# Causal and window masks of nine passes of a first attention layer added by VectorE, with a changed order of normalising

## The reference, cut to what matters

```
def masked_softmax(s, mask, sink=None):
    s = jnp.where(mask, s, -jnp.inf)
    m = jnp.max(s, axis=-1, keepdims=True)
    ...
    e = jnp.where(mask, jnp.exp(s - m), 0.0)
    den = jnp.sum(e, axis=-1, keepdims=True)
    ...
    return e / jnp.where(den > 0, den, 1.0)
```

## Time and profile before

| | us |
|---|---|
| median of three runs | 763.97 |
| lowest and highest | 763.23, 764.12 |
| the profiled execution | 764.18 |
| its span | 762.4 |

### The profile page before, as it was taken

One profiled execution on the slowest core, in us unless ns is written; L12 is line 12 of the kernel. 1 busy time (PEld: TensorE's weight loads), 2 busy tenths in 40 slices (PEclk: granted clock), 3 DMA queues, 4 the chain that ended last, 5 costly groups with the idle time before them and its releaser, 6 DMA issues.

```text
span 762.4 us, 12229 instructions
## 1 busy us (share of the span) xinstructions
PE 745.4 (98%) x5039; PEld 641.5 (84%) x5039; DVE 497.9 (65%) x685; ACT 380.3 (50%) x577; POOL 25.6 (3%) x43
## 2 busy tenths in 40 slices
PE   5999999999999999999999999999999999999998
PEld 3687876478888878788999999999878999999886
DVE  1486769638847757884889999647863735546431
ACT  2564476545354756545543444697453544344330
POOL 3000001001000000013000000000000000000000
PEclk9999999999999999999999999999999999999999
DMA  9995348914366373353745554514453654454511
GB/s 367 422 380 184 153 172 326 400 70 144 123 237 242 111 262 126 111 204 117 273 172 185 197 191 166 192 58 138 152 183 135 229 214 183 152 219 173 213 56 55
DMA packets 21959, 146.50 MB, mean 192 GB/s; under 512 B 2589, under 2 KB 2717, under 8 KB 5393
## 3 DMA queue, kind: packets, MB, share of 16 engines
q1 hardware_dynamic: 20880, 142.62, 50.4%
q0 software_dynamic: 752, 2.06, 0.9%
q10 hardware_dynamic: 272, 1.05, 0.3%
HBM read 144.68 MB, written 1.05 MB: 191 GB/s over the span
## 4 chain that ended last, share of the span: by engine, by line
PE 78%; DVE 2%; issue 2%; ACT 0%; POOL 0%; POOLq 0%; DVEq 0%; ACTq 0%
PE banks L456 23%; PE banks L458 22%; PE banks L457 22%; PE banks L550 3%; PE banks L639 1%; PE banks L574 1%; DVE WL L1686 1%; PE banks L678 1%; PE banks L646 1%; PE banks L923 0%; PE banks L908 0%; PE banks L682 0%; DVE KT L1718 0%; PE banks L927 0%; PE banks L925 0%
## 5 line engine op out<-in xcount | busy, mean ns | idle before, releaser
L1686 DVE TENSOR_TENSOR WL<-RAW,WH 128x2048 fp32r<-128x2048 f32 (+1 forms) x103 | 233.6, 2278 | 60.2 <-ACT WH L1170 59.9
L1170 ACT ACTIVATE WH<-RAW 128x2048 fp32r<-128x2048 f32 (+1 forms) x103 | 195.7, 1906 | 72.6 <-PE banks L458 65.6
L456 PE MATMUL banks<-HH,WH 128*128 128x256 f32 x768 | 217.9, 284 | 0.0
L457 PE MATMUL banks<-HL,WH 128*128 128x256 f32 x768 | 217.3, 283 | 0.0
L458 PE MATMUL banks<-HH,WL 128*128 128x256 f32 x768 | 217.3, 283 | 0.0
L457 PEld LDWEIGHTS banks<-HL,WH 128*128 128x128 f32 x768 | 147.3, 192 | 0.1
L456 PEld LDWEIGHTS banks<-HH,WH 128*128 128x128 f32 x768 | 147.3, 192 | 0.1
L458 PEld LDWEIGHTS banks<-HH,WL 128*128 128x128 f32 x768 | 147.3, 192 | 0.0
L456 PE MATMUL banks<-WH,HH 128*128 128x512 f32 (+1 forms) x320 | 127.7, 399 | 1.9 <-DVE WL L1686 0.8
L458 PE MATMUL banks<-WH,HL 128*128 128x512 f32 (+1 forms) x320 | 124.6, 389 | 0.0
L457 PE MATMUL banks<-WL,HH 128*128 128x512 f32 (+1 forms) x320 | 124.5, 389 | 0.0
(11 more groups left out here) (295 smaller groups left out, 910.6 us busy)
## 6 DMA issues: line engine op xcount, KB each, us to landing
RAW<-in_weights_dram SPq DMA_DIRECT2D x114, 1024.0 KB, 4.8
BIG<-in_weights_dram SPq DMA_DIRECT2D x6, 1024.0 KB, 6.2
ROTS<-in_weights_dram SPq DMA_DIRECT2D x4, 1024.0 KB, 7.2
PROBS<-in_weights_dram SPq DMA_DIRECT2D x2, 1024.0 KB, 11.6
RAW<-in_weights_dram SPq DMA_DIRECT2D x2, 816.0 KB, 10.3
GATE<-in_weights_dram SPq DMA_DIRECT2D x3, 512.0 KB, 9.7
X<-in_x_dram ACTq DMA_DIRECT2D x1, 1024.0 KB, 6.0
QT<-in_weights_dram SPq DMA_DIRECT2D x1, 1024.0 KB, 13.7
```

Source lines behind the costliest of these rows:

```text
L456: pe.matmul(out_, lhsT=w[0], rhs=x[0], start=start, stop=False, **more)
L457: pe.matmul(out_, lhsT=w[0], rhs=x[1], start=False, stop=False, **more)
L1170: do(act.activation(WH[:, home[n], 0:kb * width], RAW[:, slot[n] % RAW_RING, 0:kb * width], ACT.Copy), high_done)
L1686: do(dve.tensor_tensor(WL[:, home[n], w], RAW[:, slot[n] % RAW_RING, w], WH[:, home[n], w], ALU.subtract), low_done)
```

## The change

`by_vector(p)` is true for all passes but 4, 5 and 6. In those passes TensorE issues no mask matmuls: the second score matmul of each unit closes the bank. VectorE, ahead of the minimum, adds a constant of 1e30 or zero to the two diagonal blocks of both banks (128x512) in place in PSUM, and in a window pass also to the block behind the diagonal of the second half (128x256), and waits for the adds to complete. In steps 8 to 11 of layer 0, VectorE normalises pass i - 1 ahead of the minimum of pass i; in the other steps behind it, as before.

Further: `low_stick(3)` stands ahead of the split `lows(branch_first + 7)`. In front of the feed-forward VectorE makes both splits of fi0 ahead of `low_banks(3, 0)`, the first of fi1 between the two `add_merged` of the second half and the second of fi1 ahead of `stat_merged(1)`; ScalarE makes both splits of fi1 ahead of `square("n3", 1)`; TensorE turns the second half of the norm in the middle of `hidden_tokens(1, 0)` and not ahead of it.

```diff
--- before.py
+++ after.py
@@ -449,6 +449,9 @@
         block = ctx.enter_context(nc.Block())
 
 
+        def by_vector(p):
+            return p not in (4, 5, 6)
+
         @block.tensor
         def _(pe):
             def product(out_, w, x, start, stop, **more):
@@ -636,10 +639,13 @@
                         q, k = x["q"], x["k"]
                         kb = q // 2 if k is None else k
                         out_ = bank[:, 0:P] if t == 0 else bank[:, P:TRI]
-                        pe.matmul(out_, lhsT=half_of(q, QT, q // 2, t * P, (t + 1) * P),
-                                  rhs=half_of(q, KT, kb, 0, (t + 1) * P), start=(t == 0), stop=False)
-                if p == 0:
-                    pe.wait_ge(mask_set, 1)
+                        mm = pe.matmul(out_, lhsT=half_of(q, QT, q // 2, t * P, (t + 1) * P),
+                                       rhs=half_of(q, KT, kb, 0, (t + 1) * P), start=(t == 0), stop=(by_vector(p) and t == 1))
+                        if by_vector(p) and t == 1:
+                            ps.fill(mm, f"s.{u}")
+                if by_vector(p):
+                    return
+                pe.wait_ge(mask_set, 1)
                 for u, bank in zip(pair, banks):
                     window = units[u]["mask"] == "window"
                     diagonal = bank[:, 0:TRI].rearrange("p (b c) -> p b c", b=3)[:, 0:3:2, :]
@@ -991,7 +997,7 @@
             pe.wait_ge(mt_low, 4)
             output(2)
 
-            def hidden_tokens(i, t):
+            def hidden_tokens(i, t, between=None):
 
                 for half in range(2):
                     wait_parts(pe, f"fi{i}", half)
@@ -1000,6 +1006,8 @@
                 bank = ps.open(pe, "proj", use)
                 out_ = bank[:, :].rearrange("p (u c) -> p u c", u=2)
                 for k in range(KB):
+                    if between and k == KB // 2:
+                        between()
                     mm = product(out_, [h[:, k, t * P:(t + 1) * P] for h in (HH, HL)],
                                  [w[:, slot_:slot_ + 2, k * 256:(k + 1) * 256] for w in (WH, WL)], k == 0, k == KB - 1)
                 ps.fill(mm, use)
@@ -1013,8 +1021,7 @@
 
             normed(3, 0)
             hidden_tokens(0, 0)
-            norm_turn(3, 1)
-            hidden_tokens(1, 0)
+            hidden_tokens(1, 0, lambda: norm_turn(3, 1))
             normed(3)
             hidden_tokens(0, 1)
             hidden_tokens(1, 1)
@@ -1604,11 +1611,10 @@
             square("n3", 0)
             highs(first_split("fi0") + 2)
             high_norm(3, 0)
-            highs(first_split("fi1") + 1)
+            highs(first_split("fi1") + 2)
             for c in range(2):
                 ps.wait_drained(act, f"y2.1.{c}")
             square("n3", 1)
-            highs(first_split("fi1") + 2)
             high_norm(3, 1)
 
             def silu_tokens(i, t):
@@ -1845,6 +1851,14 @@
                 for u in (2 * p, 2 * p + 1):
                     ps.wait_filled(dve, f"s.{u}")
                 h = units[2 * p]["sink"]
+                if by_vector(p):
+                    diagonal = both_scores[:, :, 0:TRI].rearrange("p u (b c) -> p u b c", b=3)[:, :, 0:3:2, :]
+                    mask = const("maskw")[:, 0:P].unsqueeze(1).unsqueeze(1).to_broadcast([P, 2, 2, P])
+                    do(dve.tensor_tensor(diagonal, diagonal, mask, ALU.add))
+                    if units[2 * p]["mask"] == "window":
+                        behind_ = const("maskw")[:, P:2 * P].unsqueeze(1).to_broadcast([P, 2, P])
+                        do(dve.tensor_tensor(both_scores[:, :, P:S], both_scores[:, :, P:S], behind_, ALU.add))
+                    do.after()
                 do(dve.tensor_reduce(NM[:, pair, 0], both_scores[:, :, 0:P], AX.X, ALU.min))
                 do(dve.tensor_reduce(NM[:, pair, 1], both_scores[:, :, P:TRI], AX.X, ALU.min),
                    peaks_got if h is None else None)
@@ -1902,9 +1916,12 @@
             def attention(layer, extra):
                 a, b = spans[layer]
                 for i in range(a, b + 4):
+                    short = layer == 0 and i > 7
+                    if short and i - 1 < b:
+                        normalise(i - 1)
                     if i < b:
                         peaks(i)
-                    if a <= i - 1 < b:
+                    if not short and a <= i - 1 < b:
                         normalise(i - 1)
                     if a <= i - 3 < b:
                         heads_out(layer, i - 3)
@@ -2276,8 +2293,8 @@
             conf(2)
             low_stick(2)
             conf(3)
+            low_stick(3)
             lows(branch_first + 7)
-            low_stick(3)
             lows(branch_first + 8)
             fence[0] = FENCES["branches"]
 
@@ -2311,15 +2328,14 @@
             stat_merged(0)
             dve.wait_ge(ffnr_in, 16)
             gained_hat("n3", 0, FFNR)
-            lows(first_split("fi0") + 1)
+            lows(first_split("fi0") + 2)
             low_banks(3, 0)
-            lows(first_split("fi0") + 2)
             add_merged(1, 0)
+            lows(first_split("fi1") + 1)
             add_merged(1, 1)
-            lows(first_split("fi1") + 1)
+            lows(first_split("fi1") + 2)
             stat_merged(1)
             gained_hat("n3", 1, FFNR)
-            lows(first_split("fi1") + 2)
             low_banks(3, 1)
 
             def gate_tokens(i, t, n):
```

## The result

The changed kernel takes 765.72 us (median of 6 runs, 765.25 to 766.67), the kernel before beside it 763.6; the ratio is 1.0033, interval 1.0021 to 1.0044. So it is 0.33% slower, just over what such a measurement can tell from no change, and just above the end of my range (765.3). The profiled execution took 765.81, its span is 764.0.

A forecast was written before the change was run, and what follows sets the result against it. TensorE, busy 745.4 of 762.4 us, was taken as the bound, with VectorE work free only where nothing waits for it. The terms summed to -0.95 us, giving 763.0 us, range 761.2 to 765.3.

The forecast's parts named there:

- the sum: Whole kernel: 3.1 - 0.6 - 2.1 - 0.55 - 0.8 = -0.95 us against the kernel before.
- steps (a) to (e): Passes 0 to 3: chain passing each add's delay on until TensorE is 3.1 us late at the compressed scores.
- What a mask costs either engine: Each moved mask: TensorE saves 0.23 (causal) or 0.40 (window); VectorE's adds cost 0.73 or 1.06 us.
- layer 1: Passes 12 to 19: VectorE waits for TensorE there, so the adds are hidden and 2.1 us is gained.
- the choice of 0.23 over 0.34: Causal pass: 0.23 us saved on TensorE, not 0.34, because the first full product behind a differently tiled group is slow.
- Passes 0 to 3: First four passes, two masks each: VectorE's adds make the minimum late and the kernel 3.1 us longer.
- Passes 7 to 11: Later passes of layer 0: step 7 loses 0.3, steps 8, 10 and 11 gain, 9 nothing; -0.6 us.
- Branch outputs: ato.0 to ato.2: low_stick(3) ahead of a split removes a 1.1 us loss, of which 0.55 is kept.
- Norm before the feed-forward: Reordered splits and turn remove two TensorE waits (0.6 and 0.5); a later silu wait costs 0.3; -0.8 us.
- The third: Short steps 7 to 11 each wait for exponentials, and window passes absorb nothing: 766.2 us; chance 0.10.
- The first (adds hidden): Adds of passes 0 to 3 are hidden after all, -1.6 instead of +3.1: 758.3 us; chance 0.07.
- the second: All ends favourable outside passes 0 to 3, 0.34 saved per mask, ato keeps 1.1: 761.8 us; chance 0.23.

The follow-up runs named there:

- e13: Changed kernel with dummy transposes in TensorE's waits at the turns of passes 0, 1, 2, 5 and 6 and inside pass 2's turn: 762.87 us, ratio 0.9988.
- e3: Kernel before with only the masks of passes 0 to 3 moved to VectorE: 769.74 us, ratio 1.0071.
- e4: Kernel before with only pass 3's mask moved to VectorE: 765.95 us, ratio 1.0029.
- e2: Changed kernel with the masks of passes 0 to 3 back on TensorE: 758.47 us, ratio 0.9934.
- the tail alone: Kernel before with only the edits behind layer 1 (low_stick(3), the splits of fi0 and fi1, the moved turn): 762.04 us, ratio 0.9982.
- e11: Kernel before with 10 dummy transposes ahead of the turn of pass 6, where there was hardly a wait: 764.18 us, ratio 1.0013.

## Why the prediction failed

**The step that failed is the sum.** It added lateness and savings, each at full clock, and priced TensorE's waits at their own length. It had no term for what waits do to the granted clock: 3.0 us in the profiled execution. One line even shut it out: "As matmuls are only removed, a loss in TensorE's own time is excluded." The matmuls left took longer. By executions it is 765.7 against e13's 761.4 at full clock, 4.3, of which 1.6 are a further stretch as the profiled execution of the kernel before also has it (there from 161.6 on, from 167.0 after). I had the means: my own steps (a) to (e) said that TensorE would be idle ahead of the compressed scores, and the page of the profile shows the granted clock in a row of its own. The Trainium skill, "TensorE: Matmul & The Clock Gate", section What's actually happening, says of this clock that "the default state is throttled, and activity releases the throttle"; the windows above agree: 1.70 of 4 us busy, then 0.5. By that rule the prediction would have needed a rival "half clock behind the waits"; with what the trace shows of it, 3.0 less the 0.5 of step 6, that rival stands at 763.0 + 2.5 = 765.5. The stretch at 161.6 of the kernel before, with TensorE busy ahead of it, is not explained by that sentence.

**What a mask costs either engine**: right. Window adds 0.69 and 0.42, 1.06 with the wait. A causal add is 0.70, and 0.73 with the wait. At full clock layer 1 alone gave 2.2 for 2.1; in the trace of the changed kernel its eight passes take back 0.25, 0.28, 0.24, 0.24, 0.43, 0.24, 0.24 and 0.25, 2.2 in all. Seven of the eight lie between 0.24 and 0.28, so the choice of 0.23 over 0.34 holds: the product behind the mask comes 0.35 sooner, and its successor gives 0.1 of that back. The eighth is pass 16, with 0.43 as put; passes 7 to 10, with conditioning behind them too, saved 0.43 or 0.44 each. Only the pass with transposes behind it gave 0.28 for 0.31.

**Passes 0 to 3**: right, +3.17 for +3.1, by the steps as told. Where TensorE loses the time is only partly as told: 0.76 ahead of the rotated block's product at 82.22 and 0.39 at the turn of pass 0 instead of 0.7 ahead of the scores of pass 2; 0.82 at the turn of pass 1 for about 1; and 1.89 at that of pass 2 for about 1, since what the masks no longer cost TensorE comes out as waiting there. Nothing was to be regained in passes 4 to 6, but step 6 takes back 0.4 to 0.5 in the three traces with a slow stretch at 112 and no dummies (changed, e3, e4). E3 gave the whole chain (compressed scores at 111.25; 766.8 with one stretch of 3.4 us, 2.6 over the kernel before with one), e4 its last link, e2 its absence.

**Passes 7 to 11**: -0.67 in the trace, -0.6 alone at full clock, for -0.6. Step 7 gave +0.34 (the turn of pass 6 waits 0.74), step 8 -0.44, 10 -0.36, 11 -0.25. Step 9 came out at 0.04: it gained 0.43 and lost 0.47 to this wait, for the score bank:

```profile
153.44 0.93 PE L642 MATMUL banks<-KT,QT 64*128 64x128 f32 x8 [0.41 <-ACT PROBS L1294]
```

**Branch outputs**: -0.75 in the trace of the changed kernel, -0.53 in those of e2 and e13, for -0.55, by the mechanism told. The wait for the transformed block has gone, which gives 1.2, and ato.2 starts 0.67 later than it could. The bracket says "issue", but VectorE's read of ato.0's bank ends at 542.86, 0.1 ahead of the start. The 0.2 by which the traces differ come in the products behind it, and why isn't shown.

```profile
542.17 0.69 DVE L2265 SCALAR_TENSOR_TENSOR ROTS<-BIG,banks 128x512 f32<-128x512 f32 x1
```

```profile
542.24 0.28 PE L461 MATMUL banks<-AL,WL 128*128 128x256 f32 x1
542.96 0.36 PE L459 MATMUL banks<-AL,WH 128*128 128x256 f32 x1 [0.44 <-issue]
```

**Norm before the feed-forward**: -0.66 for -0.8. Both waits have gone, 1.2 for the 1.1 that I had put. The silu's bank is late instead, 0.62 between starts where 0.23 is usual, and the product behind it starts 0.1 later still: 0.5 for 0.3. With the branch outputs that is -1.4 for -1.35, as the tail alone gave.

```profile
582.89 0.39 PE L461 MATMUL banks<-WH,HL 128*128 128x512 f32 x1
583.51 0.47 PE L459 MATMUL banks<-WH,HH 128*128 128x512 f32 x1 [0.23 <-DVE ZT L2345]
```

**The rivals.** The third names 766.2, near the result, but mostly by a mechanism that did not happen: its wait for the exponentials came in one step, 9, while steps 8, 10 and 11 gained, and passes 0 to 3 absorbed what I said. That its number is near is luck. The first (adds hidden) and the second are out by the compressed scores and by the layer 1 rows.

**The range** was built from the ends of known terms. A whole term was missing, and all of it lies on one side.

## What to carry to other kernels

Where a change makes the busiest engine wait in a cluster, price the waits twice: their length, and the time at half clock that may follow; take the waits of one place together, not only the longest, and look at the granted clock behind them in the trace of an experiment. A part-by-part undo pays here: the same change without its four worst passes is 0.66% faster than the kernel before. And moving work to an engine with spare time helps only in the steps in which its result isn't what the next engine waits for.

## What the runs showed of the hardware that I had not expected

TensorE's granted clock fell to half behind waits that were each short: 0.39, 0.82, 1.89 and 0.41 us in the changed kernel (rows above), and 1.01 and 0.41 in e4. It then stayed there for some 6.8 us in the first case and about 3.4 in the second, although TensorE was busy throughout. Equal waits don't give equal stretches: e3 was busy for the same 1.70 of 4 us ahead, and its profiled execution has 3.4 us at half clock there and not 6.8. A stretch of 3.4 costs about 1.6 us (762.6 and 764.2 of the kernel before). The same program meets it in some executions and not in others, and one such stretch appeared in the kernel before directly behind TensorE at work without a gap. Dummy transposes in a wait kept the clock up at no cost that shows (e13, 761.4 at full clock, the sum's value), and cost 0.1 us each where there was no wait (e11).
